# A hybrid decoder trunk: score products alternate between even and odd heads, probabilities times values in two column halves

## The chip, the cores and the metric

The kernel runs on one core of a Trainium2 chip. The time is device time in microseconds (us) of that core, as a median over executions. Engines are named as the profile names them: PE (TensorE, matrix products, with PEld for its weight loads), ACT (ScalarE), DVE (VectorE), SP (it issues the DMAs here).

## What is computed

Two layers over 512 tokens of width 1024, all in float32. A layer projects the normed input into three branches (a short convolution, gated linear attention, sliding window attention), gates and mixes them, and ends in an MLP. The change concerns the sliding window branch: 8 query heads, 2 key and value heads of 64 dimensions, blocks of 128 tokens, each of which sees its own block and the one before.

```python
s = jnp.einsum('bnqkgd,bnckd->bkgnqc', qb, kw)          # scores: 128 queries by 256 keys
s = jnp.where(mask, s, -jnp.inf)
m = jnp.maximum(jnp.max(s, axis=-1, keepdims=True), sink)
p = jnp.exp(s - m)
denom = jnp.sum(p, axis=-1, keepdims=True) + jnp.exp(sink - m)
o = jnp.einsum('bkgnqc,bnckd->bkgnqd', p, vw) / denom    # probabilities times values
```

## The kernel before

The large products (projections, gates, output, MLP) are units of 128 output features: three float32r products for each tile of 128 inputs, a high and a low part of weights and activations (L410 to L412). ACT rounds the weights to the high part `wh` (L663), DVE subtracts to get the low part `wl` (L857), three units ahead; both wait for the unit that last used the buffer. They write the four `acc` banks.

The branches' small products are steps between the projection units. One list, `SEQUENCE`, gives the order of units and steps, and all engines walk it, each in order. The part that matters here:

```python
VS0 QN4 gv1 VT0 QN0 gv2 VT1 QN1 KV0 gv3 VT2 SC0 QN2 cx0 VT3 GO0 SM0 SC1 cx1 ATT2 GO1 PT0 SM1 SC2
KV1 QN3 cx2 ATT3 GO2 PV0 PT1 SM2 SC3 cx3 GO3 PV1 PT2 SM3 cc0 OSUM PV2 PT3 SC4 cc1 SM4 SC5 ON0
cc2 PV3 PT4 SM5 SC6 ON1 cc3 PV4 PT5 SM6 SC7 ON2 cb0 PV5 PT6 SM7 ON3 cb1 PV6 PT7 cb2 PV7 cb3 gr0
```

Lower case words are projection units, upper case ones steps. A layer has eight attention steps i: key head `i // 4` (`kv`), block `i % 4` (`n`), each with the four query heads of that key head. Block 0 has no block before it. A step i goes through:

- SC (L566 to L578 on PE, the product at L574): scores of four heads, an even and an odd half. The queries `sq` of an even head lie in partitions 0 to 63, of an odd one in 64 to 127, and the keys `kd` in both halves. The halves go to two banks, SCia and SCib. DVE adds the mask into `sm` (L1128), takes the maximum (L1132) and ACT the exponentials (L772).
- SM: DVE forms the reciprocal of the sum (L1142, L1144), ACT scales (L779).
- PT (L584): PE transposes the probabilities, previous and current block, ACT copies them to `pT` (L785).
- PV (L586 to L597): PE multiplies the values with `pT`. The 64 value dimensions stand twice in `vd`, so that one product of 128 stationary columns gives rows 0 to 63 and again rows 64 to 127 for all four heads (512 moving columns). Of this, two quarters are used: rows 0 to 63 of the even heads' 256 columns and rows 64 to 127 of the odd heads'. ACT copies them to `yh` (L792), DVE makes `yl` (L1153) and frees the bank.

The small steps share four other banks in turn (`open_bank` waits until the fill four before has been read), so SCib takes the bank that an earlier step's reader frees: for SC3, SC4 and SC7 that is PV0, PV2 and PV4, and ON1 takes PV3's. Other steps named below: GO and KV (gated linear attention, products on 64 rows), OSUM (32 products with one moving column, and DVE's reciprocal roots behind it), ON (rows of the norm).

Of the kernel before, what the change touches and what calls it, by code (L numbers as in the profile page):

```python
# [17 lines left out]
P = 128  # L18
# [3 lines left out]
SWA_HEADS, SWA_KV, SWA_DIM = 8, 2, 64  # L22
# [106 lines left out]
def hybrid_trunk(nc, x, positions, params, w_in, gla_wa2, w_branch, w_o, w_up, w_down, norms, consts, gmask, out):  # L129
# [3 lines left out]
    with ctx:  # L133
# [38 lines left out]
        pT = at("probs_keys", 78, [2, 4, P])  # L172
# [210 lines left out]
        def _(pe):  # L383
# [83 lines left out]
            with pe.Fori(0, DEPTH) as l:  # L467
                for word in SEQUENCE:
# [17 lines left out]
                    elif kind == "VT":  # L486
                        b = open_bank(l, word)
# [4 lines left out]
                    elif kind == "KT":  # L492
                        b = open_bank(l, word)
                        pe.wait_ge(gla_qk, l * 2 + i + 1)
                        for t in range(TT):
                            last = nc.tensor.transpose(b[:, t * P:(t + 1) * P], gk[:, i, t * P:(t + 1) * P], ident)
                        last.then_inc(bank_full, 1)
                    elif kind == "ATT":
                        b = open_bank(l, word)
                        pe.wait_ge(gla_qk, l * 2 + i // 2 + 1)  # L500
                        r = GLA_DK * (i % 2)
                        for t in range(TT):
                            s = slice(t * P, (t + 1) * P)
                            last = nc.tensor.matmul(b[:, s], kin[r:r + GLA_DK, i // 2, s], gq[r:r + GLA_DK, i // 2, s],
                                                    start=True, stop=True)
                        last.then_inc(bank_full, 1)
                    elif kind == "KV":
                        for odd in range(2):
                            b = open_bank(l, word + "ab"[odd], True, waits=[] if odd else
                                          [(kendT_ready, l * 2 + i + 1), (vT_ready, l * 4 + 2 * i + 2)])  # L510
                            r = GLA_CHUNK * odd
                            for h in range(2):
                                for t in range(TT):
                                    last = nc.tensor.matmul(  # L514
                                        b[GLA_DK * h:GLA_DK * (h + 1), t * P:(t + 1) * P],
                                        kendT[r:r + GLA_CHUNK, i, t, GLA_DK * h:GLA_DK * (h + 1)],
                                        vT[r:r + GLA_CHUNK, 2 * i + h, t, :], start=True, stop=True)
                            last.then_inc(bank_full, 1)
                    elif kind == "GO":
                        b = open_bank(l, word)  # L520
                        pe.wait_ge(att_ready, l * 4 + i + 1)
                        pe.wait_ge(vT_ready, l * 4 + i + 1)
                        pe.wait_ge(states_ready, l * 2 + i // 2 + 1)
                        r = GLA_DK * (i % 2)
                        for t in range(TT):
                            nc.tensor.matmul(b[:, t * P:(t + 1) * P], vT[:, i, t, :], attm[:, i % 2, t, :],
                                             start=t == 0, stop=False)
                        for c in range(1, CHUNKS):
                            s = slice(c * GLA_CHUNK, (c + 1) * GLA_CHUNK)
                            last = nc.tensor.matmul(b[:, s], S[r:r + GLA_DK, i // 2, c - 1, :],  # L530
                                                    gq[r:r + GLA_DK, i // 2, s], start=False,
                                                    stop=c == CHUNKS - 1)
                        last.then_inc(bank_full, 1)
                    elif kind == "QSUM":
                        b = open_bank(l, word)
                        pe.wait_ge(swa_sq, l * 5 + 5)
                        for i in range(5):
                            source = sqk[:] if i == 4 else sqr[:, i, :]
                            for t in range(TT):
                                last = nc.tensor.matmul(b[:, HEADS_Q * t + 2 * i:HEADS_Q * t + 2 * i + 2],  # L540
                                                        source[:, t * P:(t + 1) * P], blk, start=True, stop=True)
                        last.then_inc(bank_full, 1)
                    elif kind == "OSUM":
                        b = open_bank(l, word)
                        pe.wait_ge(yo_sq, l * 4 + 4)
                        for h in range(GLA_HEADS):
                            for t in range(TT):
                                last = nc.tensor.matmul(b[:, GLA_HEADS * t + h:GLA_HEADS * t + h + 1],  # L548
                                                        sqo[h][:, t * P:(t + 1) * P], ones, start=True, stop=True)
                        last.then_inc(bank_full, 1)  # L550
                    elif kind == "QN":
                        b = open_bank(l, word)
                        pe.wait_ge(wide_ready, l * 5 + QN_ORDER.index(i) + 1)
                        for t in range(TT):
                            last = nc.tensor.transpose(b[:, t * P:(t + 1) * P],
                                                       wide[i][:, t].rearrange("p h d -> p (h d)"), ident)
                        last.then_inc(bank_full, 1)
                    elif kind == "ON":
                        rows(l, word, 3, 3, lambda t: GLA_HEADS * t + i)
                    elif kind == "VS":  # L560
                        b = open_bank(l, word)
                        pe.wait_ge(sv_ready, l + 1)
                        for t in range(TT):
                            last = nc.tensor.transpose(b[:, t * P:(t + 1) * P], vtmp[:, 0, t * P:(t + 1) * P], ident)
                        last.then_inc(bank_full, 1)
                    elif kind == "SC":  # L566
                        kv, n = i // TT, i % TT
                        pe.wait_ge(swa_roped, l * 5 + 3 + 2 * kv)
                        for odd in range(2):
                            b = open_bank(l, word + "ab"[odd])  # L570
                            r = SWA_DIM * odd
                            first = 0 if n else P
                            for j in range(2):
                                last = nc.tensor.matmul(  # L574
                                    b[:, j * 2 * P + first:(j + 1) * 2 * P],
                                    sq[r:r + SWA_DIM, 2 * kv + j, n * P:(n + 1) * P],
                                    kd[r:r + SWA_DIM, kv, (n - 1) * P + first:(n + 1) * P], start=True, stop=True)
                            last.then_inc(bank_full, 1)  # L578
                    elif kind == "PT":
                        pe.wait_ge(probs_ready, l * 8 + i + 1)  # L580
                        for cur in ((0, 1) if i % TT else (1,)):
                            b = open_bank(l, word + ("cur" if cur else "prev"))
                            for h in range(4):
                                last = nc.tensor.transpose(b[:, h * P:(h + 1) * P], sm[i % 2][:, h, cur * P:(cur + 1) * P], ident)  # L584
                            last.then_inc(bank_full, 1)
                    elif kind == "PV":  # L586
                        kv, n = i // TT, i % TT
                        b = open_bank(l, word)
                        pe.wait_ge(vs_ready, l + 1)
                        if n:  # L590
                            pe.wait_ge(pprev_ready, l * 6 + kv * 3 + n)
                            nc.tensor.matmul(b[:], vd[:, kv, n - 1].rearrange("p a d -> p (a d)"),
                                             pT[:, 0].rearrange("p h c -> p (h c)"), start=True, stop=False)
                        pe.wait_ge(pcur_ready, l * 8 + i + 1)
                        nc.tensor.matmul(b[:], vd[:, kv, n].rearrange("p a d -> p (a d)"),
                                         pT[:, 1].rearrange("p h c -> p (h c)"), start=n == 0,
                                         stop=True).then_inc(bank_full, 1)  # L597
                with pe.Fori(0, N_BRANCH) as g:
                    for pos in range(GATE_IT):
                        if pos % 8 < 4:  # L600
# [692 lines left out]
```

## Time and profile before

| | us |
|---|---|
| median of 3 runs (lowest, highest) | 1733.09 (1728.52, 1734.94) |
| the profiled execution, device time | 1730.09 |
| its span | 1728.3 |
| PE busy | 1687.9 |
| DVE busy | 959.3 |
| ACT busy | 614.2 |

The span goes from the first to the last instruction of the profiled execution. PE's busy time is a union of matmuls whose ends are modelled, so it says little about how full the array is. In the rows below a float32 product shows as two matmuls (two passes), a float32r product as one. A merged line of the timeline gives the start of the first and the length until the last one ends; the end of a matmul overlaps the start of the next, so the distance between starts is what it costs PE. Stages can be told by the lines: L574 are scores, L592 and L595 PV with the previous and the current block.

### The profile page before, as it was taken

Reading aid. Unit: us, or ns where it says so; the run is one execution under the profiler, and the core shown is the slowest. Engines: PE = TensorE matmul, PEld = TensorE weight load, DVE = VectorE, ACT = ScalarE, POOL = GpSimd, SP = SyncE. Lnnn points to the kernel's source line nnn. Section 1 sums busy time; section 2 is a strip of 40 time slices with the busy share of each in tenths; the row PEclk is TensorE's granted clock in tenths of the full one; section 3 lists DMA queues with packets and bytes.
Section 4 is the critical chain, followed back from the end, with each engine's and each line's share of the span. In section 5 each row is a group of like instructions: output and inputs, shape, how many; then the busy total and the mean of one; then the engine's idle time right before and its main releaser. Section 6 shows DMA issues by size and latency. Waiting matters only on the chain.

```text
span 1728.3 us, 22648 instructions
## 1 busy us (share of the span) xinstructions
PE 1687.9 (98%) x7728; PEld 1377.5 (80%) x7728; DVE 959.3 (56%) x1399; ACT 614.2 (36%) x951; POOL 0.2 (0%) x4
## 2 busy tenths in 40 slices
PE   5999999999999999999999999999999999999997
PEld 4787778888888888888878876788888888888886
DVE  6567466544665445454655756664455654444456
ACT  5424444322334232323343344342233432323232
POOL 0000000000000000000000000000000000000000
PEclk9999999999999999999999989999999999999999
DMA  5221112332332323232222102132222333332321
GB/s 159 81 74 50 49 49 74 119 100 73 97 122 98 98 97 98 93 101 86 86 75 90 58 25 74 49 103 93 97 97 98 98 100 95 98 97 97 97 97 50
DMA packets 142806, 151.04 MB, mean 87 GB/s; under 512 B 5984, under 2 KB 135296, under 8 KB 142720
## 3 DMA queue, kind: packets, MB, share of 16 engines
q1 hardware_dynamic: 142288, 149.63, 27.0%
q8 instruction: 44, 0.72, 0.2%
q10 hardware_dynamic: 432, 0.34, 0.1%
q14 instruction: 42, 0.34, 0.1%
HBM read 147.87 MB, written 2.10 MB: 87 GB/s over the span
## 4 chain that ended last, share of the span: by engine, by line
PE 81%; DVE 9%; ACT 4%; DVEq 3%; issue 2%; ACTq 1%; DMA 0%
PE acc L410 26%; PE acc L411 25%; PE acc L412 25%; DVE wl L857 2%; ACT wh L663 2%; ACTq L709 1%; PE bank L514 1%; DVE conv_taps L1005 1%; PE bank L540 1%; ACT probs L772 1%; DVE small L1132 1%; DVEq L1131 1%; PE bank L574 0%; PE bank L548 0%; PE bank L530 0%
## 5 line engine op out<-in xcount | busy, mean ns | idle before, releaser
L410 PE MATMUL acc<-uh,wh 128*128 128x512 f32 (+1 forms) x1392 | 550.7, 396 | 5.1 <-DVE wl L857 4.9
L412 PE MATMUL acc<-uh,wl 128*128 128x512 f32 (+1 forms) x1392 | 544.7, 391 | 0.0
L411 PE MATMUL acc<-ul,wh 128*128 128x512 f32 (+1 forms) x1392 | 544.6, 391 | 0.0
L857 DVE TENSOR_TENSOR wl<-raw,wh 128x1024 fp32r<-128x1024 f32 x253 | 310.0, 1225 | 119.3 <-ACT wh L663 96.6
L663 ACT ACTIVATE wh<-raw 128x1024 fp32r<-128x1024 f32 x253 | 266.0, 1053 | 297.6 <-PE acc L412 271.5
L410 PE MATMUL acc<-yh,wh 128*128 128x512 f32 (+1 forms) x832 | 323.9, 389 | 0.6 <-DVE yl L1163 0.6
L411 PE MATMUL acc<-yl,wh 128*128 128x512 f32 (+1 forms) x832 | 323.7, 389 | 0.0
L412 PE MATMUL acc<-yh,wl 128*128 128x512 f32 (+1 forms) x832 | 323.7, 389 | 0.0
L410 PEld LDWEIGHTS acc<-uh,wh 128*128 128x128 f32 (+1 forms) x1392 | 261.4, 188 | 65.8 <-issue 9.2
L412 PEld LDWEIGHTS acc<-uh,wl 128*128 128x128 f32 (+1 forms) x1392 | 261.2, 188 | 57.8 <-issue 0.7
L411 PEld LDWEIGHTS acc<-ul,wh 128*128 128x128 f32 (+1 forms) x1392 | 261.7, 188 | 55.1 <-issue 1.0
L410 PEld LDWEIGHTS acc<-yh,wh 128*128 128x128 f32 x832 | 156.2, 188 | 33.8 <-DVE yl L1163 1.5
L412 PEld LDWEIGHTS acc<-yh,wl 128*128 128x128 f32 x832 | 156.2, 188 | 32.7
L411 PEld LDWEIGHTS acc<-yl,wh 128*128 128x128 f32 x832 | 156.2, 188 | 32.2
L1225 DVE TENSOR_TENSOR temps<-acc,rsqrt_rows_mlp 128x512 f32<-128x512 f32 x64 | 44.3, 692 | 124.6 <-PE acc L412 124.6
L1214 DVE TENSOR_TENSOR temps<-temps 128x512 f32<-128x512 f32 x64 | 44.3, 692 | 124.0 <-ACTq L823 123.5
L822 ACT ACTIVATE temps<-acc 128x512 f32<-128x512 f32 x64 | 38.4, 600 | 171.8 <-PE acc L412 171.8
L802 ACT ACTIVATE gate_tanh<-gate_tanh 128x512 f32<-128x512 f32 x48 | 30.4, 633 | 183.2 <-DVEq L1178 183.2
L1177 DVE TENSOR_TENSOR gate_tanh<-acc,rsqrt_rows 128x512 f32<-128x512 f32 x48 | 33.1, 690 | 88.2 <-PE acc L412 87.7
L1216 DVE TENSOR_TENSOR yl<-temps,yh 128x512 fp32r<-128x512 f32 x64 | 44.3, 693 | 44.7 <-ACT yh L825 44.7
L672 ACT ACTIVATE uh<-xT,norm_weights 128x512 fp32r<-128x512 f32 x40 | 28.9, 723 | 109.2 <-DVEq L1229 56.9
L857 DVE TENSOR_TENSOR wl<-raw_branch,wh 128x512 fp32r<-128x512 f32 x48 | 33.3, 693 | 56.1 <-ACT wh L663 55.7
(162 smaller groups left out, 1054.4 us busy)
## 6 DMA issues: line engine op xcount, KB each, us to landing
raw<-in_w_in_dram SPq DMA_DIRECT2D x54, 1024.0 KB, 5.2
raw<-in_w_up_dram SPq DMA_DIRECT2D x32, 1024.0 KB, 5.3
raw<-in_w_down_dram SPq DMA_DIRECT2D x32, 1024.0 KB, 4.9
raw_branch<-in_w_branch_dram SPq DMA_DIRECT2D x12, 1024.0 KB, 5.0
raw<-in_w_o_dram SPq DMA_DIRECT2D x8, 1024.0 KB, 5.0
x_tokens<-in_x_dram SPq DMA_DIRECT2D x4, 512.0 KB, 7.3
out_dram<-x_tokens SPq DMA_DIRECT2D x4, 512.0 KB, 2.7
consts<-in_consts_dram SPq DMA_DIRECT2D x1, 384.0 KB, 9.1
```

Source lines behind the costliest of these rows:

```text
L410: nc.tensor.matmul(acc[b][0:m, :], h[:, k, :], right_h(k), start=k == 0, stop=False)
L411: nc.tensor.matmul(acc[b][0:m, :], h[:, k, :], right_l(k), start=False, stop=False)
L412: return nc.tensor.matmul(acc[b][0:m, :], lo[:, k, :], right_h(k), start=False, stop=k == n - 1)
L663: nc.scalar.activation(split_view(wh, base, pos), raw_view(base, pos), ACT.Copy).then_inc(hi_done, 2 if base == 0 and pos == 0 else 1)
L672: nc.scalar.activation(uh[:, k, :], xT[:, k, :], ACT.Copy, scale=weight).then_inc(u_hi, 1)
L802: nc.scalar.activation(gt[:, pos % 4, :], gt[:, pos % 4, :], ACT.Tanh, scale=0.5).then_inc(gate_ready, 1)
L822: nc.scalar.activation(T[pos % 2], a[:], ACT.Relu).then_inc(free, 1)
L857: V.tensor_tensor(split_view(wl, base, pos), raw_view(base, pos), split_view(wh, base, pos).bitcast(f32), ALU.subtract).then_inc(lo_done, ...
L1177: V.tensor_tensor(gt[:, pos % 4, :], a[:], rs[:], ALU.mult).then_inc(free, 1)
L1214: V.tensor_tensor(t, t, t, ALU.mult).then_inc(hid_val, 1)
L1216: V.tensor_tensor(yl[:, pos, :], t, yh[:, pos, :].bitcast(f32), ALU.subtract).then_inc(hid_ready, 1)
L1225: V.tensor_tensor(T[2], a[:], rs2[:], ALU.mult).then_inc(free, 1)
```

## The change

The score products of one step alternate between the even and the odd half of the array's rows, and both banks are opened before the first. A PV product of 128 stationary and 512 moving columns becomes two of 64 stationary and 256 moving columns: values by the even heads into bank partitions 0 to 63, values by the odd heads into 64 to 127. The two quarters that nobody read are no longer computed.

```diff
                     elif kind == "SC":
                         kv, n = i // TT, i % TT
                         pe.wait_ge(swa_roped, l * 5 + 3 + 2 * kv)
-                        for odd in range(2):
-                            b = open_bank(l, word + "ab"[odd])
-                            r = SWA_DIM * odd
-                            first = 0 if n else P
-                            for j in range(2):
+                        both = [open_bank(l, word + half) for half in "ab"]
+                        first = 0 if n else P
+                        for j in range(2):
+                            for odd in range(2):
+                                r = SWA_DIM * odd
                                 last = nc.tensor.matmul(
-                                    b[:, j * 2 * P + first:(j + 1) * 2 * P],
+                                    both[odd][:, j * 2 * P + first:(j + 1) * 2 * P],
                                     sq[r:r + SWA_DIM, 2 * kv + j, n * P:(n + 1) * P],
                                     kd[r:r + SWA_DIM, kv, (n - 1) * P + first:(n + 1) * P], start=True, stop=True)
-                            last.then_inc(bank_full, 1)
+                                if j == 1:
+                                    last.then_inc(bank_full, 1)
...
+                        def weighted(odd, cur):
+                            r = SWA_DIM * odd
+                            return nc.tensor.matmul(b[r:r + SWA_DIM, 2 * odd * P:(2 * odd + 2) * P],
+                                                    vd[:, kv, n - 1 + cur, 0, :],
+                                                    pT[:, cur, 2 * odd:2 * odd + 2, :].rearrange("p h c -> p (h c)"),
+                                                    start=cur == 0 or n == 0, stop=cur == 1)
                         if n:
                             pe.wait_ge(pprev_ready, l * 6 + kv * 3 + n)
-                            nc.tensor.matmul(b[:], vd[:, kv, n - 1].rearrange("p a d -> p (a d)"),
-                                             pT[:, 0].rearrange("p h c -> p (h c)"), start=True, stop=False)
+                            for odd in range(2):
+                                weighted(odd, 0)
                         pe.wait_ge(pcur_ready, l * 8 + i + 1)
-                        nc.tensor.matmul(b[:], vd[:, kv, n].rearrange("p a d -> p (a d)"),
-                                         pT[:, 1].rearrange("p h c -> p (h c)"), start=n == 0,
-                                         stop=True).then_inc(bank_full, 1)
+                        for odd in range(2):
+                            last = weighted(odd, 1)
+                        last.then_inc(bank_full, 1)
```

## Rows read from the trace of the kernel before

**Rows 1.** The page: PE's busy time, and the chain by engine.

```profile
PE 1687.9 (98%) x7728; PEld 1377.5 (80%) x7728; DVE 959.3 (56%) x1399; ACT 614.2 (36%) x951; POOL 0.2 (0%) x4
...
PE 81%; DVE 9%; ACT 4%; DVEq 3%; issue 2%; ACTq 1%; DMA 0%
```

**Rows 2.** Groups by line and form: busy us, mean ns of one, idle before.

```profile
L574 PE MATMUL bank<-swa_k_twice,swa_q 64*128 64x256 f32 x96 | 21.2, 411 | 3.6 <-DVE yl L1153 2.4 <-DVE gla_att L1068 1.1
...
L595 PE MATMUL bank<-probs_keys,swa_v_twice 128*128 128x512 f32 x32 | 17.4, 628 | 0.0
```

**Rows 3.** Timeline of PE at PV1 and PV5: start us, length us.

```profile
178.24 1.13 PE L592 MATMUL bank<-probs_keys,swa_v_twice 128*128 128x512 f32 x2
...
180.06 1.04 PE L584 MATMUL bank<-consts,probs 128*128 128x128 f32 x8
...
231.91 1.02 PE L592 MATMUL bank<-probs_keys,swa_v_twice 128*128 128x512 f32 x2
...
233.62 1.04 PE L584 MATMUL bank<-consts,probs 128*128 128x128 f32 x8
```

**Rows 4.** The chain that ended last, in order of time.

```profile
178.31 1.06 PE bank L592 x2
...
190.05 1.16 PE bank L592 x2
...
221.32 1.07 ACT wh L663
...
294.20 0.50 PE acc L410
...
1096.72 1.07 ACT wh L663
```

**Rows 5.** Timeline of PE at ON1 and SC7, idle time in brackets.

```profile
213.54 0.65 PE L463 MATMUL bank<-consts,stat 128*128 128x128 f32 x4 [2.08 <-DVE yl L1153]
...
222.95 1.13 PE L574 MATMUL bank<-swa_k_twice,swa_q 64*128 64x256 f32 x4
...
224.88 1.13 PE L574 MATMUL bank<-swa_k_twice,swa_q 64*128 64x256 f32 x4 [0.81 <-DVE yl L1153]
```

**Rows 6.** Timeline of PE at SC5 and ON0.

```profile
201.04 1.14 PE L574 MATMUL bank<-swa_k_twice,swa_q 64*128 64x256 f32 x8
...
202.11 0.65 PE L463 MATMUL bank<-consts,stat 128*128 128x128 f32 x4
```

**Rows 7.** Timeline of PE at SC3, three narrow windows.

```profile
167.67 0.70 PE L574 MATMUL bank<-swa_k_twice,swa_q 64*128 64x256 f32 x2
...
167.99 0.59 PE L574 MATMUL bank<-swa_k_twice,swa_q 64*128 64x256 f32 x2
...
168.20 0.59 PE L574 MATMUL bank<-swa_k_twice,swa_q 64*128 64x256 f32 x2
```

**Rows 8.** Timeline of ACT, DVE and PE around PV0, PV2, SC7, PV7.

```profile
167.12 0.77 ACT L792 ACTIVATE yh<-bank 64x256 fp32r<-64x256 f32 x2
...
193.82 0.86 DVE L1153 TENSOR_TENSOR yl<-bank,yh 64x256 fp32r<-64x256 f32 x2 [0.77 <-PE bank L584]
...
225.86 1.29 DVE L1128 TENSOR_TENSOR probs<-bank,consts 128x512 f32<-128x512 f32 x2 [0.33 <-issue]
...
249.55 1.02 PE L595 MATMUL bank<-probs_keys,swa_v_twice 128*128 128x512 f32 x2
...
1042.23 0.86 DVE L1153 TENSOR_TENSOR yl<-bank,yh 64x256 fp32r<-64x256 f32 x2 [0.35 <-PE bank L574]
```

**Rows 9.** Timeline of PE at KV1: up to 153.95, and whole.

```profile
153.09 1.08 PE L514 MATMUL bank<-gla_v_tokens,gla_k_end_tokens 64*64 64x128 f32 x11
...
153.09 2.56 PE L514 MATMUL bank<-gla_v_tokens,gla_k_end_tokens 64*64 64x128 f32 x32
```

**Rows 10.** Windows: busy us (count) of PE, PEld, DVE, ACT, POOL; PEclk, DMA.

```profile
996.30:1006.40 10.10, 10.10 (x47) 8.34 (x48) 5.95 (x16) 3.87 (x13) 0.00 (x0) 0.50 0.31 101
...
190.80:194.00 3.20, 3.20 (x10) 1.85 (x9) 1.76 (x10) 0.89 (x3) 0.00 (x0) 0.50 0.22 77
```

## Prediction

> **What bounds the kernel now.** I read the page first. PE is busy 98% of the span, and 81% of the chain that ended last is PE [rows 1]. Most of that is products of the projections and the MLP, which the edit doesn't touch. What it touches, by the code: 64 score products (2 layers, 8 steps, 4 heads) and 28 products of probabilities times values (PV: 2 layers, 8 of the current block, 6 of the previous one). The groups by line count two passes for each float32 product, 32 at L595 for 16 [rows 2]. By the starts in the timeline a PV product costs PE 0.86 us: PV5, two products, starts at 231.91 and PT6 behind it at 233.62, 1.71 us later [rows 3]; a pass of 512 columns takes 0.43, one of 256 by that 0.214. All 28 are 24 us, 1.4% of the span. That is the whole stake, so the question is where in the two attention stages (in layer 1 up to about 294 us, and the same steps in layer 2) PE sets the pace.
>
> The chain of waits answers that. It is PE at PV1 and PV2, but from 221.32 it runs through ACT and DVE (a split, then yl, scores, convolution and gates), and PE comes back only at 294.20 [rows 4]. Layer 2 repeats it: at 1096.72 ACT's split is the chain [rows 4]. So PV3 (which has a 2.08 us wait for DVE right behind it [rows 5]) and PV4 to PV7 lie where PE waits anyway; of PE's time there, nothing reaches the end.
>
> **Score products.** The edit reorders even, even, odd, odd to even, odd, even, odd, and opens both banks first. Does PE overlap the row halves only when they alternate? No: SC5 in the old order took 1.14 us for all eight passes [rows 6], while in SC7, where bank b was late, four passes took 1.13 us alone [rows 5], and passes of one half start 0.32, then 0.21 us apart [rows 7]. Four steps of 0.21 hold eight passes if both halves are open. So the old order overlaps already, and the reorder is worth 0. The Trainium skill says otherwise in "TensorE: Matmul & The Clock Gate", section "Part 3: Packing small matmuls": only LDWEIGHTS is pulled ahead and MATMULs start strictly in program order. That disagrees with SC5's eight passes; what it would give is a rival below.
>
> What the open does: in SC0, SC2, SC3 and SC7 bank b is freed late; the idle time of L574's group is this wait [rows 2]. Before, the even half ran during that wait and the odd half after it, four passes; now all eight run after it, in the same time (1.13 against 1.14 us), so PE's end stays. Only the even bank is filled later. DVE's mask add follows: in SC7 it starts at 225.86, 0.98 us after bank b came free at 224.88 [rows 5, 8]. Now the even bank is full 1.13 us after that, so DVE starts 0.15 us later. SC7 is on the ACT and DVE part of the chain, so this is a loss, 0.15 a layer, 0.3 us in all. Behind that add wait the maximum, ACT's exponentials and the next split on DVE. Bounds: 0 if a gap elsewhere absorbs it, 1.13 us a layer if DVE had nothing else to do first. In SC0, SC2 and SC3 DVE has splits and SM steps in front of its add, and PE is the chain behind them: 0.
>
> **Probabilities times values.** Each product of 128 stationary columns and 512 moving ones becomes two of 64 and 256: 28 become 56, passes 56 become 112. Their length halves to the 0.21 us of the score's 256 columns [rows 7]. If they run one after the other nothing is won; if the column halves overlap, a pair takes 0.21 a pass. KV shows that form of neighbour: 64 by 64 tiles, first eight passes into the lower bank partitions, then eight into the upper, from the same array rows. Eleven passes had started by 153.95, within 0.86 us, where 0.107 us a pass (half of 0.214, for half the columns) would allow eight, and all 32 took 2.56 us instead of 3.4 [rows 9]. The second column half therefore starts before the first is done. PV's halves are only two passes apart, nearer than KV's eight. I take full overlap; the other end is none.
>
> The new shape changes the array's tiling. The eight score passes take 1.07 us from their first start to the next operation's, where four steps of 0.214 are 0.86: 0.21 goes to the unhidden first load and to leaving [rows 6, 7]. Entering I put at 0.1 (an estimate: half of that; 0 to 0.21). The Trainium skill's "TensorEngine Tiling (Array Packing)", section "Tiling Modes", says that a change of tiling mode drains the engine; the trace agrees. It gives no duration, so by it alone no sum follows.
>
> Per step, then. PV2, 3, 5, 6, 7: before 1.71, after 4 x 0.214 + 0.21 + 0.1 = 1.17, saves 0.54. PV1 follows tiled GO products, so it already pays to enter: before 178.24 to 180.06, 1.82; after 1.07; saves 0.75 [rows 3]. PV0 (one product, after GO): 0.86 and the 0.11 that PV1 shows over PV5, to 2 x 0.214 + 0.21 = 0.64, saves 0.33. PV4: 0.86 to 0.74, saves 0.12. Sum 3.9 us a layer, 7.8 us of PE time.
>
> How much arrives:
> PV1, both layers: PE is the chain before and behind; all of it, 2 x 0.75 = 1.5 us.
> PV2: its bank goes to ACT's copy and DVE's L1153, and SC4 waits for that. In layer 1 DVE had idled 0.77 us before L1153, in layer 2 only 0.35, about the gap between any two of its steps (its reciprocal roots after OSUM run until then) [rows 8]. So 0.42 of the 0.54 can arrive in layer 1, none in layer 2: 0.4 us.
> PV0: ACT starts its copy with no idle time before it, busy with GO2's squares; SC3 then waits for DVE [rows 8]. 0; up to 0.33 a layer if not.
> PV3 to PV6: PE only waits longer, at ON1, SC7b, PV7 and 294.20. 0.
> PV7: its second product started at 249.55 [rows 8], behind ACT's copy of PT7; PE isn't the chain. 0.
> Sum: 1.5 + 0.4 - 0.3 = 1.6 us. The profiled execution (1730.09, of it 1728.3 the span) would become 1728.5. The median of the runs lies 3.0 above it, at 1733.09; the forecast is 1733.1 - 1.6 = 1731.5 us.
>
> No copy, DMA, bank or semaphore count changes. The cover for the 6 us that don't arrive is ACT and DVE; were it gone, all 7.8 would count.
>
> **Rivals.**
> A, PE bounds after all: the ACT and DVE chain from 221 us moves up with PE. For it: PE 98% busy. Against: the chain, and the waits of PE. All 7.8 us arrive: 1725.3. With free mode changes it would be 28 x 0.43 = 12 us, 1721.1.
> B, the clock. This is the other side. In layer 2 the granted clock was 0.50 (1.2 of 2.4 GHz) from 996.3 to 1006.4, just after SC2's wait for its second bank, while layer 1 kept full clock at that place; another such stretch of over 3.2 us follows the thin products of OSUM [rows 10]. The edit lengthens exactly these silences: in SC0, SC2 and SC7 PE now stands still for the even half's time too, and at ON1 for what PV3 saves. Price: half the stretch, 5 us if layer 1's KV1 gets what layer 2 has, 1.6 us for a short one. One short one on PE's part of the chain cancels the gain; the long one gives 1736.5.
> C, the column halves don't overlap at 128 rows. A PV step of two products is then 8 x 0.214 + 0.21 + 0.1 = 2.02, 0.31 longer; PV1 1.92, 0.10 longer. On the chain: 2 x 0.10 + 0.31 for PV2 in layer 1 + 0.3 for SC7 = 0.8 slower, 1733.9; up to 1735 if PV0 and layer 2's PV2 count.
> D, MATMULs start only in program order, the Trainium skill's rule. Then alternation gives what the old order could not: four steps of 0.214, 0.86 us, in each 256 column group, and 0.43 in SC4; on PE's part of the chain are SC2, SC3, SC4, 2.15 us a layer, 4.3 in all: 1727.2. Against it stand the 1.14 us of SC5.
>
> **How the numbers follow.** Forecast 0.57, A 0.08, B 0.15, C 0.15, D 0.05. A measurement of this kernel can tell about 0.5% (8.7 us) from no change: the bounds are 1724.4 and 1741.8. The forecast, D and C lie inside; of A about half goes beyond, and B needs several stretches. Faster 0.06, same 0.89, slower 0.05. Range 1725 to 1738: down to A's 1725.3, up over C and B's long stretch with 1.5 us for a second one; the runs before spread over 6 us by themselves.
>
> **What would show it.** PV1 from its first start to PT2's about 1.07 us; PV5 about 1.17; PV passes of 64 columns in flight in pairs. SC5 still 1.14; SC0, SC2 and SC7 as one group of eight with the old end. The waits at ON1 and before 294 longer by what PE saved. L1128 of SC7 about 0.15 later against its bank's release. Wrong if PV takes 2 us (C), if the chain between 221 and 294 turns to PE (A), or if a half clock stretch stands where none did (B).

## The result: slower by 0.25%, at a lower clock

The changed kernel takes 1736.02 us (median of 20 runs, 1731.91 to 1740.47) beside 1731.38 for the kernel before (20 runs, 1727.0 to 1736.39): ratio 1.0025, 95% interval 1.0014 to 1.0036. The forecast was 1731.5 with a range of 1725 to 1738 and a gain of 1.6 us. The time lies in the range, but the sign is wrong.

This is from the page of the changed kernel. PE is busy 13 us less, near the 28 x 0.43 = 12 us that the PV passes lose in length, and the span isn't shorter:

```profile
span 1730.1 us, 22770 instructions
...
PE 1675.1 (97%) x7784; PEld 1369.9 (79%) x7784; DVE 958.9 (55%) x1399; ACT 614.3 (36%) x951; POOL 0.2 (0%) x4
...
PE 82%; DVE 8%; ACT 4%; DVEq 2%; issue 2%; ACTq 1%; DMA 0%
```

The steps themselves, in the timeline of PE (start us, length us). PV is L593 now, PT L585. These answer to [rows 3]:

```profile
179.84 1.08 PE L593 MATMUL bank<-probs_keys,swa_v_twice 128*64 128x256 f32 x8
...
180.86 1.09 PE L585 MATMUL bank<-consts,probs 128*128 128x128 f32 x8
...
233.89 0.39 PE L412 MATMUL acc<-uh,wl 128*128 128x512 f32 x1
...
234.21 1.08 PE L593 MATMUL bank<-probs_keys,swa_v_twice 128*64 128x256 f32 x8
...
235.22 1.10 PE L585 MATMUL bank<-consts,probs 128*128 128x128 f32 x8
...
236.16 0.60 PE L463 MATMUL bank<-consts,stat 128*128 128x128 f32 x4
```

PV1 costs 1.02 us from its start to PT2's (forecast 1.07, before 1.82). For PV5, take the last product of the unit before it: 233.89 to the row of ON3 behind PT6 at 236.16 is 2.27 us. The same distance before was 231.68 to 234.49, 2.81 us:

```profile
231.68 0.39 PE L412 MATMUL acc<-uh,wl 128*128 128x512 f32 x1
...
234.49 0.60 PE L463 MATMUL bank<-consts,stat 128*128 128x128 f32 x4
```

So PV5 saves 0.54, the forecast to the digit: eight passes in 1.01 instead of 1.71, then 0.09 for entering the narrow form (0.32 from the last unit product to the first pass, 0.23 before) and 0.07 more in the transposes behind. The column halves do overlap: rival C is out.

The score steps and their readers, in the timelines of PE and DVE (idle time in brackets; the mask add is L1135 now), beside [rows 5, 6, 8]:

```profile
153.56 1.13 PE L574 MATMUL bank<-swa_k_twice,swa_q 64*128 64x256 f32 x8 [1.65 <-DVE gla_att L1075]
...
203.26 1.13 PE L574 MATMUL bank<-swa_k_twice,swa_q 64*128 64x256 f32 x8
...
204.33 0.65 PE L463 MATMUL bank<-consts,stat 128*128 128x128 f32 x4
...
215.76 0.86 PE L463 MATMUL bank<-consts,stat 128*128 128x128 f32 x4 [2.64 <-DVE yl L1160]
...
227.11 1.14 PE L574 MATMUL bank<-swa_k_twice,swa_q 64*128 64x256 f32 x8 [1.99 <-DVE yl L1160]
...
228.28 1.29 DVE L1135 TENSOR_TENSOR probs<-bank,consts 128x512 f32<-128x512 f32 x2 [0.51 <-PE bank L574]
...
296.60 0.50 PE L410 MATMUL acc<-uh,wh 128*128 128x512 f32 x1 [0.42 <-DVE wl L864]
```

SC5 takes 1.07 us to the next step's start, as before. SC2 and SC7 are groups of eight behind a longer silence. In SC7 the mask add comes 1.17 us after bank b (228.28 - 227.11), 0.19 later than the 0.98 before; the forecast was 0.15. It reaches the end of the stage: from bank b of SC7 to PE's return to the chain it is 69.49 us (227.11 to 296.60), before 69.32 (224.88 to 294.20). PE waits 2.64 us at ON1 (2.08 before), and at 296.60 it waits 0.42 us for `wl`: what PV3 to PV7 saved went into waits, as said.

PV2 has its reader behind OSUM. Before, layer 1's L1153 started at 193.82 [rows 8], 7.39 us after OSUM's start; now the same operation (L1160) starts 6.96 us after it, 0.43 earlier (forecast 0.42):

```profile
186.43 0.72 PE L548 MATMUL bank<-consts,squares_o 128*128 128x1 f32 x6
```

```profile
187.26 3.63 PE L548 MATMUL bank<-consts,squares_o 128*128 128x1 f32 x32
...
194.22 0.86 DVE L1160 TENSOR_TENSOR yl<-bank,yh 64x256 fp32r<-64x256 f32 x2 [0.35 <-issue]
```

That looks like the forecast saving, but it isn't one of the new form. Before, layer 1's PV2 ran partly at half clock (from 190.80 on [rows 10]), and so its reader was late. Where the old form ran at full clock, DVE's own work set this start already: 6.96 us behind OSUM's start in layer 2 of the kernel before (from 1035.27 to the 1042.23 of [rows 8]), and 6.98 us in layer 1 of e3_late_signal, a run below with the old PV form:

```profile
1035.27 3.63 PE L548 MATMUL bank<-consts,squares_o 128*128 128x1 f32 x32
```

```profile
191.26 3.63 PE L548 MATMUL bank<-consts,squares_o 128*128 128x1 f32 x32
...
198.24 0.86 DVE L1153 TENSOR_TENSOR yl<-bank,yh 64x256 fp32r<-64x256 f32 x2 [0.35 <-issue]
```

At full clock PV2 therefore saves nothing, and the sum would be 1.5 - 0.3 = 1.2 us. The terms of PV1 and SC7 are there within 0.05 us.

What isn't in the sum is the clock. Here are stretches at the 1.2 GHz level in the changed kernel (busy us and count of PE, PEld, DVE, ACT, POOL, then the granted clock):

```profile
192.00:199.00 7.00, 5.30 (x22) 4.22 (x22) 4.12 (x16) 2.18 (x5) 0.00 (x0) 0.51 0.12 39
...
216.00:219.40 3.40, 3.40 (x11) 2.72 (x10) 2.85 (x5) 1.70 (x4) 0.00 (x0) 0.51 0.00 0
...
997.70:1007.90 10.20, 10.20 (x50) 8.51 (x47) 6.76 (x16) 3.74 (x13) 0.00 (x0) 0.50 0.25 87
...
1038.80:1042.00 3.20, 3.20 (x16) 2.04 (x16) 1.93 (x11) 0.76 (x2) 0.00 (x0) 0.50 0.67 238
...
1062.70:1066.00 3.30, 3.30 (x11) 2.72 (x10) 2.77 (x5) 1.71 (x4) 0.00 (x0) 0.50 0.00 0
```

Before, the stretches 190.80 and 996.30 stood at 0.50 too [rows 10], and so did ON1 of layer 1; but OSUM and ON1 of layer 2 ran at full clock:

```profile
214.80:218.00 3.20, 3.20 (x9) 2.49 (x8) 2.62 (x6) 1.44 (x4) 0.00 (x0) 0.50 0.00 0
...
1038.00:1045.00 7.00, 6.09 (x33) 4.42 (x34) 4.41 (x18) 1.95 (x4) 0.00 (x0) 1.00 0.37 129
...
1062.00:1067.00 5.00, 5.00 (x25) 4.21 (x26) 3.85 (x9) 2.58 (x7) 0.00 (x0) 1.00 0.00 0
```

Two profiles don't show that the change made these stretches, for they come and go at one and the same place. From 96 to 104 us, ahead of every step that the change touches, the clock was 0.79 before:

```profile
96.00:104.00 8.00, 8.00 (x38) 6.71 (x37) 3.60 (x13) 2.71 (x5) 0.00 (x0) 0.79 0.03 3
```

and 0.57 in the changed kernel:

```profile
96.00:104.00 8.00, 8.00 (x30) 6.86 (x31) 3.60 (x13) 1.91 (x4) 0.00 (x0) 0.57 0.00 0
```

In e3_late_signal, with the old PV form, ON1 of layer 2 stood at half clock as well, and so did KV1 of layer 1, behind a silence of 0.57 us, no longer than before:

```profile
152.50:162.70 10.20, 10.20 (x48) 8.36 (x47) 6.12 (x16) 3.87 (x13) 0.00 (x0) 0.51 0.29 96
1060.50:1063.50 3.00, 3.00 (x9) 2.32 (x8) 2.76 (x6) 1.36 (x4) 0.00 (x0) 0.50 0.00 0
```

What such a stretch costs, two executions of one kernel show. In the first profile of the changed kernel KV1 of layer 1 ran at full clock (a window's row, then the timeline of PE):

```profile
152.50:162.70 10.20, 9.14 (x67) 7.78 (x68) 7.54 (x22) 4.67 (x15) 0.00 (x0) 1.00 0.34 105
...
163.18 1.16 PE L504 MATMUL bank<-gla_q,gla_k_in 64*128 64x128 f32 x8
```

In the second, r1_after, it ran at half clock (the same, the window's row last):

```profile
152.04 2.03 PE L574 MATMUL bank<-swa_k_twice,swa_q 64*128 64x256 f32 x8 [1.67 <-DVE gla_att L1075]
...
166.41 1.16 PE L504 MATMUL bank<-gla_q,gla_k_in 64*128 64x128 f32 x8
...
152.50:162.70 10.20, 10.20 (x53) 8.52 (x50) 5.99 (x15) 3.87 (x13) 0.00 (x0) 0.52 0.28 97
```

From SC2's first pass to ATT3's (L504) it is 14.37 us instead of 9.62 (163.18 - 153.56), with the same work: 4.75 us for some 10 us of half clock. This is the long stretch of rival B, at the place and near the price (5 us) that B gave.

Over the span the profiled executions had a mean granted clock of 0.990 before and 0.987 now. Every timed run has such a mean, and many runs settle what single profiles can't: 97 different runs of the kernel before (in the three sets of comparisons below) have a mean of 0.9873, the 20 runs of the changed one 0.9833. At two levels, a mean c is 2 x (1 - c) of the span at the lower one: 44 us before, 58 us now.

### The profile page after: what moved, and what is told of

The parts are those of the page before. It is cut to its first block, busy times and chain, and to the rows that moved or that the text cites. A ratio compares the mean times of both kernels' runs of the same rounds, so it can differ in the third digit from the quotient of the medians.

```text
span 1730.1 us, 22770 instructions
## 1 busy us (share of the span) xinstructions
PE 1675.1 (97%) x7784; PEld 1369.9 (79%) x7784; DVE 958.9 (55%) x1399; ACT 614.3 (36%) x951; POOL 0.2 (0%) x4
## 4 chain that ended last, share of the span: by engine, by line
PE 82%; DVE 8%; ACT 4%; DVEq 2%; issue 2%; ACTq 1%; DMA 0%
PE acc L410 26%; PE acc L412 26%; PE acc L411 26%; DVE wl L864 2%; ACT wh L670 1%; PE bank L514 1%; ACTq L716 1%; PE bank L540 1%; PE bank L574 1%; DVE conv_taps L1012 1%; DVE small L1139 1%; DVEq L1138 0%; ACT probs L779 0%; PE bank L548 0%; PE bank L530 0%
```

## How the experiments are read

The runs of the kernel before spread over 13 us, those of the changed one over 9, and they do so with their clock: a straight line through the 97 runs of the kernel before (time against mean clock, correlation -0.89) gives 1732.9 us at 0.987 and 1.2 us more for each 0.001 of clock less. So each kernel gets two numbers: its mean clock, and how far its runs lie off that line, an estimate of what its work costs at the same clock. Errors are standard errors of the mean; the line's own error isn't in them.

| kernel | runs | median us | ratio to before (95%) | mean clock | off the line, us |
|---|---|---|---|---|---|
| before | 97 | 1731.86 | 1 | 0.9873 | 0 |
| changed (first set) | 20 | 1736.02 | 1.0025 (1.0014 to 1.0036) | 0.9833 ± 0.0005 | -1.5 ± 0.3 |
| r1_after | 12 | 1736.30 | 1.0020 (1.0007 to 1.0033) | 0.9834 ± 0.0007 | -1.2 ± 0.5 |
| e1_sc_only | 12 | 1734.18 | 1.0013 (0.9994 to 1.0032) | 0.9864 ± 0.0008 | -0.5 ± 0.8 |
| e2_pv_only | 12 | 1733.22 | 1.0007 (0.9991 to 1.0023) | 0.9841 ± 0.0010 | -3.1 ± 0.5 |
| e3_late_signal | 12 | 1730.54 | 1.0004 (0.9991 to 1.0016) | 0.9882 ± 0.0006 | +0.6 ± 0.3 |
| e4_even_twice | 12 | 1730.62 | 0.9989 (0.9976 to 1.0003) | 0.9873 ± 0.0005 | -2.1 ± 0.3 |
| e5_pv12 | 12 | 1732.17 | 1.0006 (0.9987 to 1.0025) | 0.9848 ± 0.0009 | -1.9 ± 0.3 |
| e6_pv_twice | 12 | 1735.02 | 1.0016 (1.0002 to 1.0030) | 0.9852 ± 0.0006 | -1.1 ± 0.3 |
| e7_fill | 12 | 1728.25 | 0.9973 (0.9960 to 0.9987) | 0.9896 ± 0.0004 | -1.7 ± 0.3 |
| e8_pv_not2 | 12 | 1732.50 | 1.0000 (0.9982 to 1.0017) | 0.9860 ± 0.0010 | -1.6 ± 0.3 |
| e9_half_wide | 12 | 1734.87 | 1.0013 (0.9999 to 1.0027) | 0.9828 ± 0.0006 | -3.3 ± 0.4 |
| e10_after_fill | 6 | 1723.99 | 0.9950 (0.9932 to 0.9968) | 0.9917 ± 0.0002 | -3.2 ± 0.3 |
| e11_fill_osum | 12 | 1730.56 | 0.9984 (0.9970 to 0.9998) | 0.9893 ± 0.0006 | +0.2 ± 0.3 |

The changed kernel's row is the answer in short: by the line its work is worth -1.5 us (forecast -1.6), its clock costs 0.0040 x 1210, 4.8 us; the sum is +3.3, and the means of the runs differ by 3.4 (the medians of its own set by 4.6).

That the clock moves the time, and isn't merely lower in runs that are slow for another reason, is shown by the two executions of KV1 above and by the fillers below. How much it moves it isn't known that well. The 32 runs of the changed kernel alone give 0.9 us for each 0.001; between them and e10_after_fill it is 1.4 (12.0 us for 0.0084), and e10 lies 1.9 us lower off the line than the changed kernel though it does more work, which no saving can explain. With 0.9 to 1.4 instead of 1.2 the changed kernel's work comes out between -0.1 and -2.1 us. The sign of the clock's part doesn't depend on this, the share of each part does.

## The experiments

**The halves of the change.** r1_after is the changed kernel again.

> The changed kernel again, as the yardstick beside its halves. Measured so far 0.25% (4.6 us) over the kernel before. Theory clock: the mean granted clock of its profile again lies below that of before (0.987 against 0.990, which at two levels is 45 us of half clock against 36), and about half of the difference is the loss. Theory late bank (the even bank is filled 0.15 to 0.9 us later in SC0, SC2, SC3, SC4, SC7): the loss stands at full clock too. Theory PV form (64 column passes cost more than they look): the loss is in the PV steps.

> Only the score edit, PV as before. Clock: PE stands still longer in SC0, SC2, SC3, SC4 and SC7, so some more half clock; 1 to 3 us slower. Late bank: 0.3 us from SC7, up to 2 us slower, with the granted clock of before. PV form: equal to before within 0.1%.

> Only the PV edit, scores as before. Clock: 1.9 us less on the chain (PV1 twice 0.75, PV2 0.4), against it some half clock where PE's dense work behind OSUM is shorter; between 2 us faster and 3 us slower, with the sign following the granted clock. Late bank: 1.9 us faster. PV form: all of the loss, 4 us slower or more.

e1_sc_only takes the diff's first hunk, e2_pv_only its second. r1_after repeats the loss at 0.9834. The score edit alone loses 0.0009 of clock, no more than its error, and its time is uncertain. The PV edit alone has the gain in its work (-3.1 us, even more than the 1.9 that I gave it) and loses 0.0032 of clock, 3.9 us by the line; the two cancel to 1.0007. So the PV form isn't dear. The lost clock of the halves adds up to that of the whole, and more of it comes with the PV edit, though the difference (0.0023 ± 0.0013) isn't firm. The halves' work doesn't add up: -0.5 and -3.1 beside -1.5.

**PE busy in the silences.** The even half is computed once before bank b is opened, into its place, and again behind it:

```diff
-                        both = [open_bank(l, word + half) for half in "ab"]
+                        both = [open_bank(l, word + "a")]
+                        for j in range(2 if i in (0, 2, 3, 4, 7) else 0):
+                            nc.tensor.matmul(both[0][:, j * 2 * P + first:(j + 1) * 2 * P],
+                                             sq[0:SWA_DIM, 2 * kv + j, n * P:(n + 1) * P],
+                                             kd[0:SWA_DIM, kv, (n - 1) * P + first:(n + 1) * P], start=True, stop=True)
+                        both.append(open_bank(l, word + "b"))
```

> The changed kernel, but in SC0, SC2, SC3, SC4 and SC7 the even half is also computed once before bank b is opened, in its final place, and then computed again with the odd half: PE works in the silence as before, the even bank is still signalled late. Clock: fewer half clock stretches, 1 to 3 us faster than the changed kernel. Late bank: as slow as the changed kernel.

Its timeline at SC2: four passes in the silence, then the eight at the time at which the changed kernel had them (153.56):

```profile
151.87 1.13 PE L572 MATMUL bank<-swa_k_twice,swa_q 64*128 64x256 f32 x4
...
153.60 1.14 PE L579 MATMUL bank<-swa_k_twice,swa_q 64*128 64x256 f32 x8 [0.60 <-DVE gla_att L1080]
```

Useless work, and 5.7 us less than the changed kernel's median; the clock is back at 0.9873. It signals the even bank as late as the changed kernel does, so the late bank isn't the loss. It also has the whole PV edit and the silences of e2_pv_only at the score steps, and yet 0.0031 ± 0.0011 more clock than that; nothing here explains this, so how the loss divides between the halves stays open.

**The late bank by itself.** The old order, both counts with the last odd pass:

```diff
-                            last.then_inc(bank_full, 1)
+                        last.then_inc(bank_full, 2)
```

> The kernel before, with one change: PE computes the scores in the old order, during the wait, but signals both banks with the last odd pass. DVE sees the even bank late as in the changed kernel, PE has no new silence. Theory late bank: slower than before by 0.3 us or more at the same granted clock, up to 2 us. Theory clock: within 0.3 us of before, granted clock as before (0.987 mean over runs).

```profile
228.12 1.13 PE L574 MATMUL bank<-swa_k_twice,swa_q 64*128 64x256 f32 x4 [1.22 <-DVE yl L1153]
...
229.29 1.29 DVE L1128 TENSOR_TENSOR probs<-bank,consts 128x512 f32<-128x512 f32 x2 [0.51 <-PE bank L574]
```

DVE's mask add of SC7 is 1.17 us behind bank b's passes' start here too (229.29 - 228.12), and the work is 0.6 ± 0.3 us off the line (my term was 0.3). The clock isn't lower than before (0.9882). A small cost, of the size forecast.

**Where the PV edit loses its clock.** The new form only in PV1 and PV2, and everywhere but in PV2:

```diff
+                        if i in (1, 2):          # e8_pv_not2: if i != 2:
...
+                        else:
...
```

> The kernel before with the new PV form only in PV1 and PV2, where PE is the chain. By the steps of the prediction this keeps the whole 1.9 us (twice 0.75 and 0.4) of the PV edit and saves nothing elsewhere. Clock: the clock of before, or a little lower behind OSUM; 1 to 2 us faster than before. If the narrow form itself costs clock: no faster than the form everywhere.

> New PV form in all steps but PV2, old score order. PV2 follows the thin products of OSUM, and its dense passes in the old form are what PE does there. If the clock of the PV edit is lost behind OSUM, the mean granted clock returns from 0.984 towards 0.987 and the time is about 1.5 us below before (PV1 twice). If it is lost in many places alike, the clock stays near 0.985.

e5's work lies 1.9 ± 0.3 us under the line. That fits PV1 (twice 0.75) with or without PV2 (0.4). But no time is won, for its clock is 0.9848. e8's -1.6 is PV1's 1.5; its clock of 0.9860 lies between before and e2, closer to before by 0.0006 only, with errors of 0.0010. That PV2's place behind OSUM is a part of the loss isn't shown by this.

**Missing work or narrow shape?** e6 issues the previous block's products twice; e9 keeps the old shape and computes only the even heads' 256 columns, so it leaves out the odd heads:

```diff
-                            nc.tensor.matmul(b[:], vd[:, kv, n - 1].rearrange("p a d -> p (a d)"),
-                                             pT[:, 0].rearrange("p h c -> p (h c)"), start=True, stop=False)
+                            nc.tensor.matmul(b[:, 0:2 * P], vd[:, kv, n - 1].rearrange("p a d -> p (a d)"),
+                                             pT[:, 0, 0:2].rearrange("p h c -> p (h c)"), start=True, stop=False)
```

> The new PV form everywhere, old score order, but the products of the previous block (of the current one in block 0) are issued twice, the first result being overwritten, so that PE is busy nearly as long as before the change (1.6 us a step of two products instead of 1.17). If the lost clock of the PV edit comes from the missing work, the mean granted clock returns from 0.984 towards 0.987 and the time is at most that of the PV edit alone. If it comes from the narrow shape, the clock stays at 0.984 or lower and the time is 1 us more.

> The kernel before, with PV products of the old shape (128 stationary columns) but only 256 moving columns, those of the even heads; the odd heads' result is left out. PE works even a little less in PV than in the changed kernel (0.86 us a step of two products instead of 1.02 to 1.17), and no column tiling occurs. Missing work as the cause of the lost clock: mean granted clock 0.984 as with the PV edit. Narrow shape as the cause: clock 0.987 as before, and 2.5 to 3 us faster than before.

The previous block's product of PV5 in e9's timeline, two passes in 0.59 us with the old shape:

```profile
239.71 0.59 PE L592 MATMUL bank<-probs_keys,swa_v_twice 128*128 128x256 f32 x2
```

e9 has no narrow form at all and a clock as low as the changed kernel's, 0.9828 ± 0.0006. Less work in PV is enough to lose it. e6, at 0.9852, went a third of the way that I expected (from 0.9841 to 0.987), no more than the errors, and it pays for the repeats. Its PV5 fills 1.45 us where the old form took 1.71 (L584 is PT in this kernel):

```profile
230.13 1.52 PE L592 MATMUL bank<-probs_keys,swa_v_twice 128*64 128x256 f32 x12
...
231.58 1.10 PE L584 MATMUL bank<-consts,probs 128*128 128x128 f32 x8
```

So it gives back only a part of the work, and whether the rest is that or the narrow shape stays open.

**PE's silences filled.** Products of the next unit go into that unit's own bank, which the unit then overwrites with its first product:

```diff
+            FILLER = {0: 5, 2: 3, 3: 1, 4: 2, 7: 4}        # e10_after_fill: {0: 7, 2: 6, 3: 4, 4: 4, 7: 8}
+            def fill(l, word, count):
+                at = next(w for w in SEQUENCE[SEQUENCE.index(word):] if w in UNIT)
+                pos = UNIT[at]
+                open_unit(l, 0, 0, pos)
+                for k in range(count):
+                    nc.tensor.matmul(acc[pos % 4][:], split_view(wh, 0, pos)[:, k % KT, :], uh[:, k % KT, :],
+                                     start=True, stop=True)
...
+                        if i == 1:
+                            fill(l, word, 10)              # before ON1; e10_after_fill: 11
...
+                            if odd and i in FILLER:
+                                fill(l, word, FILLER[i])
                             b = open_bank(l, word + "ab"[odd])
```

> New PV form, old score order, and PE's silences are filled: before bank b of SC0, SC2, SC3, SC4, SC7 and before ON1 it computes 5, 3, 1, 2, 4 and 10 products of the next unit into that unit's bank, which the unit then overwrites. Nothing else reads them. Theory clock: the half clock stretches behind ON1, SC7 and at KV1 go, mean granted clock 0.989 or more, 2 to 4 us faster than before. Rivals: the added products cost time where PE is the chain and the result is no faster than the PV edit alone.

> The changed kernel as it is, plus products of the next unit into its own bank in front of bank b of SC0, SC2, SC3, SC4, SC7 (7, 6, 4, 4, 8 of them) and of ON1 (11). The late signal of the even bank stays. Theory clock: mean clock 0.988 or more instead of 0.983, 4 us or more faster than the changed kernel, faster than before. If the late even bank were the loss, it would stay at 1736.

> The kernel with filled silences (new PV form, old score order), and in the middle of OSUM's 32 thin products four dense ones of the next unit: 0.9 us of PE time a layer on the chain. If the half clock stretch behind OSUM goes, up to 5 us less half clock in each layer where it stood, so 0 to 2 us faster than the kernel without it. If it stays, 1.8 us slower than that.

e7 (old score order) is 0.27% faster than before, e10 (the changed kernel as it is, with more filler; six runs) 0.50%, 12.3 us under the changed kernel's 1736.30. The fillers stand where PE stood still, at SC2 and ON1 of layer 1 in e10:

```profile
151.68 1.63 PE L475 MATMUL acc<-uh,wh 128*128 128x512 f32 x6
...
153.58 1.14 PE L590 MATMUL bank<-swa_k_twice,swa_q 64*128 64x256 f32 x8 [0.27 <-DVE gla_att L1091]
...
211.38 2.79 PE L475 MATMUL acc<-uh,wh 128*128 128x512 f32 x11
...
214.10 0.65 PE L463 MATMUL bank<-consts,stat 128*128 128x128 f32 x4
```

and the stretches around ON1, at half clock in both layers of the changed kernel, are at full clock now; behind OSUM it stays at 0.50 in both layers (layer 1 shown, layer 2 from 1031.80 to 1035.00):

```profile
192.10:195.30 3.20, 3.20 (x13) 2.35 (x11) 2.07 (x9) 1.71 (x4) 0.00 (x0) 0.50 0.16 52
...
210.00:220.00 10.00, 10.00 (x51) 7.64 (x49) 6.18 (x13) 6.13 (x18) 0.00 (x0) 1.00 0.01 2
...
1050.00:1062.00 12.00, 12.00 (x67) 8.94 (x64) 7.32 (x14) 7.89 (x23) 0.00 (x0) 1.00 0.00 1
```

e10 computes nothing new and takes nothing away: 80 more matmul passes, a clock of 0.9917 instead of 0.9834, and 12 us less. The fillers in the kernel before, without either edit, weren't run; so how much of the 0.50% needs the edits isn't known. e11 adds four products to e7 in the middle of OSUM. Its clock didn't rise (0.9893 against 0.9896), and its work is 1.9 us dearer than e7's, the 1.8 expected for that case. Its single profile shows no half clock stretch behind OSUM, but the mean over 12 runs gained nothing.

## Why the prediction was wrong

Right, with their sizes: PV1's saving on PE's chain (0.77 us from PV1's start to OSUM's in layer 1, 7.42 instead of 8.19, for the 0.75 forecast), that PV3 to PV7 go into waits, that the old order overlaps the row halves already (SC5 1.07 in both), full overlap of the column halves (e2, and 1.01 us for eight passes), the price of the change of form (0.16 in and out beside the first load), the late even bank (0.19 for 0.15, e3 +0.6 ± 0.3 for 0.3). At the same clock the forecast of -1.6 us stands against -1.5 ± 0.3 and -1.2 ± 0.5, if the line's slope is right. PV2's 0.4 was wrong, though: it compared a PV2 at half clock (layer 1) with DVE's own pace, and at full clock the old form is no later (6.96 us behind OSUM's start). The full clock value of the sum is 1.2, which the runs cannot tell from 1.6; that the forecast is met to 0.1 us is luck.

The step that failed is "How the numbers follow", with its input in rival B. B was named with its mechanism, its places and its price, and given 0.15, as a mishap that may come. The sum has no term for the clock, that is, the clock stood in it at nothing, and the runs put it at 4.8 us: 44 us of half clock on average before, 58 in the 32 runs of the changed kernel. I treated the clock as fixed and the saving as certain, when the saving on a chain that PE doesn't bound is itself silence: about 6 of the 7.8 us of freed PE time, by my own sum, were to become waits. That less PE work there lowers the clock, e9 shows; that work in the waits gives it back, e4, e7 and e10 show; what decides whether a stretch comes in one execution isn't known. B's price for its long stretch was right (4.75 us for 5, KV1 of layer 1 in r1_after). That the mean loss has the same size is luck: it is a mean over stretches of 3 to 10 us that come and go in many places, in the kernel before too. And B named mainly the longer waits of the score edit; the runs of the halves put the larger part on the PV edit (e2 against e1), without being able to settle it (e4).

Rival A is out (from 223.55 the chain runs through ACT and DVE again; PE is back at 296.60), C by the timeline, D by SC5.

## What to carry to other kernels

Ask of each saving on PE not only whether it reaches the end, but what stands in its place if it doesn't: between other engines' waits, less work on PE can mean a lower clock for the work that counts. Don't read such a loss from two profiles, for half clock stretches come and go from one execution to the next; take the mean clock over many runs. Where a run's mean clock is known, compare kernels at the same clock as well as by their medians; here the one says -1.5 us, the other +4.6, and both are needed. And where PE waits anyway, useless products that nobody reads can be worth more than the edit (12.3 us, 0.7%, in e10), as long as they stand in a wait; e11's four on the chain cost 1.9 us and gave nothing back.

## What the runs showed of the hardware

A step's matmuls can start before the last one of the step ahead of it: in the changed kernel SC1's first score pass starts at 140.48 and GO0's last pass (L530, 64 rows too) at 140.58, although it stands ahead in the program:

```profile
140.48 0.48 PE L574 MATMUL bank<-swa_k_twice,swa_q 64*128 64x256 f32 x1
...
140.58 0.27 PE L530 MATMUL bank<-gla_q,gla_states 64*128 64x64 f32 x1
```

So passes don't all start in the program's order, and alternating by hand gave nothing here: SC5 takes 1.07 us in either order. Two column halves of 128 rows run side by side in float32: eight passes of 256 moving columns in 1.01 us, where one after another would be 8 x 0.214 = 1.71. A half clock stretch also stands where PE had no idle time at all: from 96 to 104 us PE was busy 8.00 of 8.00 us at 0.79 and 0.57; what ran just before were products with only two moving columns (L540):

```profile
93.35 3.63 PE L540 MATMUL bank<-consts,squares 128*128 128x2 f32 x32
```

And 0.001 of mean clock, 3.5 us of half clock, costs the kernel before 1.2 us by the line, less than the 1.7 that half of it would be if every such moment lay on PE's chain.
